# Two chunks with a state between in mLSTM, and stacked key halves in attention

## The reference, cut to what matters

```python
# attention, per head; m runs over the two maps
s = jnp.einsum('bqhmd,bkhmd->bhmqk', qi, k) * scale
p = jax.nn.softmax(s, axis=-1)
a = p[:, :, 0] - lam * p[:, :, 1]
o = jnp.einsum('bhqk,bkhd->bqhd', a, v)

# mLSTM, one direction, one chunk
s = jnp.einsum('bhtd,bhsd->bhts', qc, kc) * w_intra
num = w_inter[..., None] * jnp.einsum('bhtd,bhde->bhte', qc, C) + jnp.einsum('bhts,bhse->bhte', s, vc)
den = w_inter * jnp.einsum('bhtd,bhd->bht', qc, n) + jnp.sum(s, axis=-1)
h = num / jnp.maximum(jnp.abs(den), jnp.exp(-m_row))[..., None]
C_new = carry_w[..., None, None] * C + jnp.einsum('bhs,bhsd,bhse->bhde', w_s, kc, vc)
n_new = carry_w[..., None] * n + jnp.einsum('bhs,bhsd->bhd', w_s, kc)
```

## Time and profile before

| what | value |
|---|---|
| median of 3 runs | 1748.39 us (1747.43 to 1749.07) |
| the profiled execution | 1748.54 us, span 1746.8 us |
| granted TensorE clock, mean | 0.994 |
| PE busy | 1696.8 us, 97% |
| DVE busy | 1097.0 us, 63% |
| ACT busy | 696.4 us, 40% |
| POOL busy | 631.4 us, 36% |
| chain that ended last | PE 74%, DVE 9%, ACT 5%, POOL 4% |

### The profile page before, as it was taken

One profiled execution on the slowest core, in us unless ns is written; L12 is line 12 of the kernel. 1 busy time (PEld: TensorE's weight loads), 2 busy tenths in 40 slices (PEclk: granted clock), 3 DMA queues, 4 the chain that ended last, 5 costly groups with the idle time before them and its releaser, 6 DMA issues.

```text
span 1746.8 us, 30132 instructions
## 1 busy us (share of the span) xinstructions
PE 1696.8 (97%) x11450; PEld 1594.1 (91%) x11450; DVE 1097.0 (63%) x1775; ACT 696.4 (40%) x1134; POOL 631.4 (36%) x317
## 2 busy tenths in 40 slices
PE   7999999899999999999999999999999999999996
PEld 4888888598989999889998899998999999999996
DVE  4776777757876515767458554644878861487824
ACT  3455555527332212232246554554463331233324
POOL 2222111356442333323454222124745333333444
PEclk9999999999999999999999999999999999999998
DMA  9322222521444213543221112211212222222221
GB/s 358 136 65 73 62 62 81 207 85 46 190 176 161 97 57 121 183 181 129 83 70 55 64 55 75 71 49 49 91 37 72 72 90 69 70 72 72 86 84 60
DMA packets 59770, 170.97 MB, mean 98 GB/s; under 512 B 7945, under 2 KB 20489, under 8 KB 59665
## 3 DMA queue, kind: packets, MB, share of 16 engines
q1 hardware_dynamic: 51584, 163.33, 26.8%
q10 hardware_dynamic: 8080, 6.18, 1.1%
HBM read 161.07 MB, written 4.74 MB: 95 GB/s over the span
## 4 chain that ended last, share of the span: by engine, by line
PE 74%; DVE 9%; ACT 5%; POOL 4%; issue 4%; DVEq 3%; DMA 1%; ACTq 1%; SPq 0%; POOLq 0%
PE pj L765 58%; POOL wlo L623 3%; PE mO L1280 2%; ACT pr L1631 2%; PE psO L1020 2%; PE pfrow L790 1%; PE psS L985 1%; DVEq L2385 1%; PE st_va L765 1%; POOL ss L637 1%; DVE pr L2399 1%; PE mO L765 1%; PE st_mu L765 1%; DVE sm L2384 1%; PE mS L1236 1%
## 5 line engine op out<-in xcount | busy, mean ns | idle before, releaser
L593 POOL TENSOR_TENSOR wlo<-wraw,whi 128x1024 fp32r<-128x1024 f32 (+1 forms) x116 | 301.9, 2603 | 739.7 <-ACT whi L1422 739.7
L765 PE MATMUL pj<-Hh,whi 128*128 128x320 f32 x2192 | 521.3, 317 | 2.2 <-POOL wlo L623 0.9
L765 PE MATMUL pj<-Hh,wlo 128*128 128x320 f32 x2192 | 504.9, 309 | 0.0
L765 PE MATMUL pj<-Hl,whi 128*128 128x320 f32 x2192 | 502.7, 310 | 0.0
L765 PEld LDWEIGHTS pj<-Hh,whi 128*128 128x128 f32 x2192 | 364.8, 188 | 28.5 <-issue 22.8
L765 PEld LDWEIGHTS pj<-Hh,wlo 128*128 128x128 f32 x2192 | 368.1, 188 | 0.3
L765 PEld LDWEIGHTS pj<-Hl,whi 128*128 128x128 f32 x2192 | 367.5, 188 | 0.4
L1422 ACT CAST whi<-wraw 128x1024 fp32r<-128x1024 f32 (+1 forms) x168 | 187.2, 1114 | 265.2 <-PE pj L765 227.7
L2295 DVE SCALAR_TENSOR_TENSOR fcv<-fus,vec,fcv 128x127 f32<-128x127 f32 (+1 forms) x176 | 206.4, 1214 | 14.4 <-issue 13.8
L1428 ACT COPY fus<-pj 128x640 f32<-128x640 f32 x84 | 58.3, 696 | 382.9 <-PE pj L765 382.9
L2157 DVE SCALAR_TENSOR_TENSOR X<-pj,mods,X 128x128 f32<-128x128 f32 (+5 forms) x114 | 43.1, 434 | 207.4 <-PE pj L765 207.3
(11 more groups left out here) (374 smaller groups left out, 2414.2 us busy)
## 6 DMA issues: line engine op xcount, KB each, us to landing
wraw<-in_w_up SPq DMA_DIRECT2D x84, 512.0 KB, 3.5
fwr<-in_w_ada SPq DMA_DIRECT2D x56, 512.0 KB, 5.7
wraw<-in_w_dn SPq DMA_DIRECT2D x32, 704.0 KB, 4.1
wraw<-in_w_qkv SPq DMA_DIRECT2D x24, 512.0 KB, 3.5
wraw<-in_w_mlin SPq DMA_DIRECT2D x24, 512.0 KB, 3.4
awr<-in_w_ada SPq DMA_DIRECT2D x16, 512.0 KB, 10.4
awr<-in_w_ada SPq DMA_DIRECT2D x16, 256.0 KB, 7.9
wraw<-in_w_wo SPq DMA_DIRECT2D x8, 512.0 KB, 3.5
```

The source lines that it names most:

```text
L593: nc.gpsimd.tensor_tensor(wlo[k][:, 0:width], wraw[k][:, 0:width], whi[k][:, 0:width].bitcast(F32), ALU.subtract).then_inc(w_lo, 1)
L765: last = mm(out[:, c, 0:HALF], w, x[:, j, c * HALF:(c + 1) * HALF], start=(j == 0 and n == 0), stop=(j == n_k - 1 and n == 2))
```

## The change

Two things are changed together.

In attention, Q's high part is written twice for each map, into both halves of the rows (Qd, one tile for each map), and K's tile for a map holds K's high part in that map's own rows and K's low part in the other ones (Ks). One matmul over 128 rows ("stacked") then makes high by high plus high by low; a second one over 64 rows ("low_query") adds low by high. A latent block has 8 matmuls instead of 12, the context block 4 instead of 6. ACT copies Q's high part four times and K's (and the cache's) twice, each on 64 rows; DVE's subtractions for Ql and Kl become two each, on 64 rows.

In mLSTM, the 512 latents become two chunks of 256. A block's scores run over its own chunk's 256 keys and over both states' normalisers (132 columns), four tiles are transposed instead of six, and the two latent parts of m_values have 24 matmuls instead of 36. Between the chunks stands a state, made once per head and direction: DVE finds the chunk's maximum (m_state_max) and weighs the keys (m_keys), ACT makes the weights (m_state_weights) and casts (m_keys_hi, m_state_hi), PE transposes the weighed keys (four more in m_turn_k) and multiplies them by the values (m_update, 12 matmuls), and DVE adds the old state (m_state_sum) and splits it (m_state_lo). Some semaphores and buffers are shared to make room.

The diff, cut to its core:

```diff
 def scores(h, st):
-                for at, k0, k1, m in spans:
-                    r = slice(DK * m, DK * (m + 1))
-                    if i < 4 and at == 640:
-                        pe.wait_ge(sc_part, 4 * h + i + 1)
-                    for n, (q, kk) in enumerate(((Qh, Kh), (Qh, Kl), (Ql, Kh))):
-                        last = mm(psS[:, at:at + k1 - k0], q[par][r, q0:q0 + P], kk[par][r, k0:k1],
-                                  start=(n == 0), stop=(n == 2))
+                def stacked(at, k0, k1, m):
+                    mm(psS[:, at:at + k1 - k0], Qd[par][m][:, q0:q0 + P], Ks[par][m][:, k0:k1], start=True, stop=False)
+
+                def low_query(at, k0, k1, m):
+                    return mm(psS[:, at:at + k1 - k0], Ql[OWN[m], q0:q0 + P], Ks[par][m][OWN[m], k0:k1], start=False, stop=True)
...
+                    wide, tail = (0, L0, L0 + 512, 0), (512, L0 + 512, KW, 0)
+                    left, right = (640, L0, L0 + 384, 1), (1024, L0 + 384, KW, 1)
+                    stacked(*tail)
+                    stacked(*right)
+                    low_query(*tail).then_inc(sc_part, 1)
+                    low_query(*right)
+                    stacked(*wide)
+                    pe.wait_ge(sc_part, 4 * h + i + 1)
+                    stacked(*left)
+                    low_query(*left)
+                    last = low_query(*wide)
 def q_hi(n):
-                nc.scalar.copy(Qh[n % 2][:, :], h32[0][:, :]).then_inc(qk_hi, 1)
+                for m in range(2):
+                    last = nc.scalar.copy(Qd[n % 2][m][OWN[m], :], h32[0][OWN[m], :])
+                last.then_inc(qk_hi, 1)
+                for m in range(2):
+                    nc.scalar.copy(Qd[n % 2][m][OTHER[m], :], h32[0][OWN[m], :])
 def q_lo(n):
-                tt(Ql[n % 2][:, :], h32[0][:, :], Qh[n % 2][:, :].bitcast(F32), ALU.subtract).then_inc(qk_ready, 1)
+                for m in range(2):
+                    r = OWN[m]
+                    last = tt(Ql[r, :], h32[0][r, :], Qd[n % 2][m][r, :].bitcast(F32), ALU.subtract)
+                last.then_inc(qk_ready, 1)
 def k_lo(n):
-                tt(Kl[par][:, 0:L0 + LAT], h32[1][:, 0:L0 + LAT], Kh[par][:, 0:L0 + LAT].bitcast(F32),
-                   ALU.subtract).then_inc(qk_ready, 1)
+                for m in range(2):
+                    k_, r = Ks[par][m], OWN[m]
+                    last = tt(k_[OTHER[m], 0:L0 + LAT], h32[1][r, 0:L0 + LAT], k_[r, 0:L0 + LAT].bitcast(F32), ALU.subtract)
+                last.then_inc(qk_ready, 1)
 def m_turn_k(h):
+                pe.wait_ge(state_keys, 3 * h + 1)
                 m_wait(("k", h))
-                nc.tensor.transpose(flatT[:, 0:P], h32[1][:, C0:C0 + CTX], ident[:, :]).then_inc(mt_full, 1)
+                for c in range(4):
+                    nc.tensor.transpose(flatT[:, c * P:(c + 1) * P], kws[:, c // 2, (c % 2) * P:(c % 2 + 1) * P], ident[:, :])
+                nc.tensor.transpose(flatT[:, 4 * P:5 * P], h32[1][:, C0:C0 + CTX], ident[:, :]).then_inc(mt_full, 1)
+
+            def m_update(h):
+
+                pe.wait_ge(mt_free, MUSE["k", h] + 1)
+                pe.wait_ge(mv_lo, 2 * h + 2)
+                m_wait(("u", h))
+                for d in range(2):
+                    for n, (k_, v_) in enumerate((k_, v_) for c in (2 * d, 2 * d + 1)
+                                                 for k_, v_ in ((kTh[:, c, :], mVh[:, c, :]), (kTh[:, c, :], mVl[:, c, :]),
+                                                                (kTl[:, c, :], mVh[:, c, :]))):
+                        last = mm(mT[:, d, 0:MDV], k_, v_, start=(n == 0), stop=(n == 5))
+                last.then_inc(mt_full, 1)
 def m_values(h, part):
-                        terms = [(mVh[:, c, dv], mVl[:, c, dv], mAh[:, c, :], mAl[:, c, :]) for c in range(4)]
-                        terms += [(mCh[:, d, dv], mCl[:, d, dv], mAh[:, 4 + d, :], mAl[:, 4 + d, :]) for d in range(2)]
+                        keys = ((0, 0), (1, 1)) if part == 1 else ((2, 0), (3, 1))
+                        terms = [(mVh[:, c, dv], mVl[:, c, dv], mAh[:, t, :], mAl[:, t, :]) for c, t in keys]
+                        states = ((0, 2), (3, 3)) if part == 1 else ((2, 2), (1, 3))
+                        terms += [(mCh[:, c, dv], mCl[:, c, dv], mAh[:, t, :], mAl[:, t, :]) for c, t in states]
+            def m_state_max(h):
...
+                for d in range(2):
+                    nc.vector.tensor_reduce(mref[:, d:d + 1], spread[:, d, d * HL:(d + 1) * HL], AX.X, ALU.max)
+                dve.drain()
+                tt(mref[:, 0:2], mref[:, 0:2], m0, ALU.max)
+                dve.drain()
+                ts(mref[:, 2:4], mref[:, 0:2], -1.0, None, ALU.mult)
+                tt(mref[:, 4:6], m0, mref[:, 0:2], ALU.subtract).then_inc(state_max, 1)
```

More of the change, by code:

```diff
@@ L254, in hybrid_step @@
             KW = TP + PAST
-            Qh, Ql, Kh, Kl = ([] for _ in range(4))
+            Qd, Ks = [], []
             with ExitStack() as g:
@@ L2001, in gate_exps @@
                 act.wait_ge(gate_steps, MAX_ROWS)
[L2002 to L2003 removed]
+                for i in range(2):
+                    t = slice(L0 + HL * i, L0 + HL * (i + 1))
+                    fn(gr[4][:, t], gr[3][:, t], ACT.Exp, scale=-1.0, bias=gm0[0:GR, 1 + i:2 + i])
                 fn(gr[4][:, 0:L0], gr[3][:, 0:L0], ACT.Exp, scale=-1.0)
@@ new lines, in m_keys @@
+            def m_keys(h):
+                n0 = vec[:, V_N0:V_N0 + 2 * ML_HEADS].rearrange("p (d h) -> p d h", d=2)[:, :, h]
+                dve.wait_ge(state_casts, 3 * h + 1)
+                for d in range(2):
+                    t = L0 + HL * d
+                    last = stt(out=kws[:, d, :], in0=h32[1][:, t:t + HL], scalar=KSCALE, in1=kws[:, d, :], op0=ALU.mult,
+                               op1=ALU.mult, accum_out=nsum[:, d:d + 1])
+                last.then_inc(state_keys, 1)
+                tt(nsum[:, 2:4], n0, mref[:, 6:8], ALU.mult)
+                dve.drain()
+                tt(nsum[:, 2:4], nsum[:, 2:4], nsum[:, 0:2], ALU.add)
+                dve.drain()
+                for d in range(2):
+                    ts(mKh[:, NC + 2 - d:NC + 3 - d], nsum[:, 2 + d:3 + d], 1.0, None, ALU.mult)
+                dve.drain()
+                for d in range(2):
+                    c = slice(NC + 2 - d, NC + 3 - d)
+                    last = tt(mKl[:, c], nsum[:, 2 + d:3 + d], mKh[:, c].bitcast(F32), ALU.subtract)
+                last.then_inc(state_keys, 1)
@@ new lines, in m_state_sum, with m_state_lo @@
+            def m_state_sum(h):
+                dve.wait_ge(mt_full, MUSE["u", h] + 1)
+                for d in range(2):
+                    last = stt(out=c0[:, d, :], in0=c0[:, d, :], scalar=mref[:, 6 + d:7 + d], in1=mT[:, d, 0:MDV],
+                               op0=ALU.mult, op1=ALU.add)
+                last.then_inc(mt_free, 1)
+            def m_state_lo(h):
+                dve.wait_ge(state_casts, 3 * h + 3)
+                tt(mCl[:, 2:4, :], c0[:, :, :], mCh[:, 2:4, :].bitcast(F32), ALU.subtract).then_inc(state_keys, 1)
```

205 lines of the change are left out of this document (128 added, 77 removed).

## The result

The changed kernel takes 1799.36 us (median of 4 runs, 1798.65 to 1800.01) against 1748.08 for the kernel before: a ratio of 1.0297, 95% interval 1.0284 to 1.0309. It is slower, as forecast, by 51 us where 38 were forecast, and 4 us above the range. The profiled execution spans 1797.3 us.

A forecast was written before the change was run, and what follows sets the result against it. PE was taken as the bound, busy 1696.8 of 1746.8 us. From 1748.5, +28.8 for boundary waits, +12 for the clock, -3 for score blocks and 0 for mLSTM gave 1786 us; range 1754 to 1795.

The forecast's parts named there:

- waits at the boundaries: At attention's head boundaries, DVE's added low parts, POOL's hold and ACT's copies make PE's row sums wait: +28.8 us.
- clock: After the waits at seven boundaries, PE runs at the lower 1.2 GHz level, 1.7 us each: +12 us.
- score blocks: In attention, 8 matmuls instead of 12 save 0.1 us in each of 32 latent blocks: -3 us.
- mLSTM: In the mLSTM heads, 13 us less PE work is given back as waits at head starts: taken as 0.
- The bound and the place: PE bounds the kernel; DVE's low parts between Ah and the row sums (rms) are on the path without slack.
- The race: At a head boundary, K's second low half on DVE starts at Ql + 2.80 us, against POOL's weight operation at 2.78.
- lost: POOL starts first and holds K's second half; Vl and rms come 3.81 us late; 1786 us in all, chance 0.48.
- won: K's second half starts ahead of POOL; Vl and rms come 1.67 us late; 1768 us in all, chance 0.28.
- ACT's copies: Four copies of Q's high part delay POOL, then K's rotation, so Ql starts 0.56 us late per boundary.

The follow-up runs named there:

- kl_ahead: Changed kernel with the cached keys' and values' low parts moved behind the values' low part on DVE: 1770.27 us, ratio 1.0127.
- before_split: Kernel before, with DVE making the low parts of Q, cached K and K in two 64-row operations each instead of one: 1790.14 us, ratio 1.0253.
- filler5: Changed kernel with 5 more matmuls of 496 columns, results unused, ahead of the row sums at six boundaries: 1790.57 us, ratio 1.0247.
- no_switch: Changed kernel with low-query matmuls over all 128 rows, each directly behind the stacked matmul of its columns: 1800.58 us, ratio 1.0303.

## Why the prediction was wrong in size and right in kind

| term | forecast, us | measured, us |
|---|---|---|
| waits at the boundaries (DVE, POOL, with ACT's 0.56) | +28.8 | 27.8 + 3.7 - 1.0 = +30.5 |
| clock | +12 | 13.6 - 1.7 = +11.9 |
| score blocks | -3 | +7.5 |
| mLSTM | 0 | 0 to +2 |
| sum | +38 | +50 to +52 |

That the measured terms add up to the 51 us is in part luck: 1.4 us of the clock's term lie within a wait and cost nothing, and the last head's four blocks, some 0.4 us longer each, are not counted.

**The bound and the place**: right. rms had no slack, and the loss lies there.

**The race**: right; "lost" is what happened at all boundaries, and kl_ahead and before_split show it by taking the cause away and by putting it alone where it was not. The working was less exact than its sum. K's second half came to its start not at Ql + 2.80, 20 ns behind POOL, but at Ql + 3.43 (265.39 - 261.96), 0.65 behind POOL's start, so it was never close, and "won" did not deserve 0.28. The paces were too short: 64x640 is issued every 0.82 us and 64x128 every 0.30, where the earlier trace rows has 0.73 and 0.20 for 128 rows, since all of these operations but the first start only when the one ahead has ended. POOL was then held by the first half of K in turn (2.83 us where it takes some 2.4) and ended at Ql + 5.6 instead of 5.15. The lateness of 3.81 us does not follow from the terms shown either. From Vl's start in the kernel before,

```profile
272.22 0.69 DVE L2445 TENSOR_TENSOR Vl<-psT,Vh 128x512 fp32r<-128x512 f32 x1
```

which is Ql + 1.87, to a release at Ql + 5.15 it is 3.3. A held operation of 640 columns doesn't end with POOL, as line 2396 with its one column did, but 0.68 us later; Vl came at Ql + 6.32, 4.45 late. The forecast of 4.4 a boundary was met, but not from its own parts.

**ACT's copies**: the mechanism was seen, as the small operation on the maxima is free and the rotation held:

```profile
252.92 0.17 DVE L2458 TENSOR_SCALAR sm<-sm 128x2 f32<-128x2 f32 x1
...
254.68 1.67 DVE L2493 TENSOR_TENSOR sx<-sx,rope 128x512 f32<-128x512 f32 x1
```

But a gain of 0.56 a boundary could not be had by moving the copies or leaving them out (+3 and -0.2 us). The term was inside the waits of DVE and ACT around it, not beside the rest.

**The clock**: right, 1.6 to 2.1 us at each of the seven boundaries; filler5 shows that the wait is its cause. For the "won" case, two thirds of it were a wrong guess: with 1.6 us of waiting in kl_ahead it does not fall.

**The score blocks**: this is the step that failed. I took -0.1 us a block from a time of 1.25 between bounds of 1.17 and 1.4, with +0.1 for a change of row form. (From these bounds follow -6 and +2 us; the end of +5 was set wider without a reason given.) A block is 1.66 to 1.78, mean 1.72, against 1.36 and the 0.09 ahead of it: +0.27 in each of 28, +7.5 us, beyond the upper bound of +5. The price of a change was worked out from the one gap at a block's start, and from a block in which all matmuls had the same form; no row showed what a mix costs inside one. The rows after tell it now: two stacked matmuls of 128 and 256 columns with the change behind them take 0.31 us, where they stream in 0.18 at the 0.12 for 256 columns of the earlier trace rows. Over the block it is 1.66 us against the 0.96 that my sum had for the streaming alone: 0.7 for four changes, where I had allowed 0.2 in all. The Trainium skill's rule, that a change of tiling mode drains TensorE ("TensorEngine Tiling (Array Packing)", Key Properties), agrees with these rows; I had put what it makes of the term near zero. That such a block is longer is shown, but not that 7.5 us would go with it: no_switch shortens the blocks by more than that and gains nothing, as waits for DVE and ACT and a longer stretch of the lower clock take it back. So the step failed twice: the term had the wrong sign (+7.5 for -3), and a shorter block would not have been a saving either, since DVE and ACT set nearly the same pace beside PE. The sum counts what PE did, not what each change would give back.

**mLSTM**: right, by the named waits in part. PE waited 3.4 us for the copy of v0 that stood behind the state's weights on ACT, lost some 2.6 to the clock behind that (at the lower level up to 1072.11, with the wait over at 1066.90), and waited 1.6 for the keys; two rows of PE show it:

```profile
PE pj L778 <- ACT h32t L1472: 3.4, 1, 3.4
...
PE mT L1288 <- DVE kws L2802: 1.6, 1, 1.6
```

I had looked for the wait at m_turn_k, where it was the smaller. The range ended 4 us too low for two reasons: the scores passed their upper bound by 2.5 us, and the top of 1795 was lower than its own bounds give (1786 + 8 + 4 = 1798).

## What to carry to other kernels

A change that takes matmuls away must not be paid in operations of an engine that the next stage waits for: three subtractions split by rows cost 44 us where 3 us of matmul time were forecast to be had in the scores. Before adding work to DVE beside POOL, ask which operation POOL's next one will hold, and put one there that nobody needs soon; the place of three operations was worth 29 us. Count changes of row form on TensorE as work, and a saving on one engine as a saving of the run only where no other engine has the same pace.
